# A pad of 224 bytes behind the small parameters of a hybrid decoder step

## What is computed

```python
h = rmsnorm(x, p['norm1_g']) * (1.0 + sc1[:, None]) + sh1[:, None]
mo, st = mixer(h, tuple(s[l] for s in states), lb_all[l], p)   # h @ w_in, three head groups, @ w_out
x = x + gt1[:, None] * mo
h = rmsnorm(x, p['norm2_g']) * (1.0 + sc2[:, None]) + sh2[:, None]
x = x + gt2[:, None] * peer(h, p['peer_wq'], p['peer_k1'], p['peer_k2'], p['peer_u'], p['peer_v'])
```

```python
act = jax.nn.gelu(jnp.einsum('thkd,td->thk', jnp.take(u, idx, axis=0), xb).astype(jnp.float32))
return jnp.einsum('thk,thkd->td', (gw * act).astype(xb.dtype), jnp.take(v, idx, axis=0))
```

## The kernel before

| tensor | start | modulo 64 | modulo 512 |
|---|---|---|---|
| x_res | 16512 | 0 | 128 |
| ring | 25728 | 0 | 128 |
| parts | 38016 | 0 | 128 |
| keep | 50304 | 0 | 128 |
| small | 52160 | 0 | 448 |
| mod | 54560 | 32 | 288 |
| gain, cond, rms, sel | 56288 to 59040 | 32 | |
| big | 63648 | 32 | 160 |
| x_parts, h_parts, act_parts, extra_ring, onehot | 210592 | 32 | 160 |
| more_ring | 214688 | 32 | 160 |

## Time and profile before

### The profile page before, as it was taken

The page is one execution under the profiler, slowest core; times in us unless marked ns, Lnnn a source line. Parts: engine busy times, 40 slices in busy tenths (PEclk is TensorE's granted clock), DMA queues, the critical chain, the costliest instruction groups (busy, mean ns, idle before and its releaser), DMA issues. The chain is left out here.

```text
span 2366.9 us, 58299 instructions
## 1 busy us (share of the span) xinstructions
PE 2266.2 (96%) x20478; PEld 2076.5 (88%) x20478; DVE 1494.1 (63%) x3095; ACT 1268.8 (54%) x2439; POOL 1054.6 (45%) x960
## 2 busy tenths in 40 slices
PE   6989999999999999999999799999999999999998
PEld 4955869999998799999989367799999978999997
DVE  3746636963225968888666664299432288787885
ACT  3533215567557955555556322165665587555554
POOL 0010106884446746566300210088644475665661
PEclk8978999999999999999999779999999999999999
DMA  7475034555552079899545821455555502898992
GB/s 281 155 280 201 3 131 164 178 181 202 188 189 92 6 264 312 287 301 312 194 171 170 310 101 38 137 185 178 199 183 187 188 33 91 295 312 275 312 312 100
DMA packets 123806, 455.40 MB, mean 192 GB/s; under 512 B 13744, under 2 KB 14256, under 8 KB 122544
## 3 DMA queue, kind: packets, MB, share of 16 engines
q1 hardware_dynamic: 105264, 386.80, 45.9%
q0 software_dynamic: 18432, 67.12, 10.3%
HBM read 449.37 MB, written 4.49 MB: 192 GB/s over the span
## 5 line engine op out<-in xcount | busy, mean ns | idle before, releaser
L426 POOL TENSOR_TENSOR parts<-ring,parts 128x512 fp32r<-128x512 f32 x358 | 463.9, 1298 | 472.0 <-ACT parts L419 457.6
L419 ACT ACTIVATE parts<-ring 128x512 fp32r<-128x512 f32 x620 | 389.2, 632 | 348.4 <-PE ps_u L473 280.5
L469 PE MATMUL ps_u<-h_parts,parts 128*128 128x256 f32 x4096 | 563.5, 280 | 0.9 <-ACT parts L419 0.6
L2649 PE MATMUL ps_y<-act_parts,parts 128*128 128x256 f32 x4096 | 563.0, 279 | 0.0
L469 PEld LDWEIGHTS ps_u<-h_parts,parts 128*128 128x128 f32 x4096 | 514.4, 188 | 3.1 <-ACT parts L419 1.7
L2649 PEld LDWEIGHTS ps_y<-act_parts,parts 128*128 128x128 f32 x4096 | 515.1, 188 | 0.7 <-ACT parts L2589 0.3
L426 DVE TENSOR_TENSOR parts<-ring,parts 128x512 fp32r<-128x512 f32 x262 | 180.6, 692 | 372.8 <-ACT parts L419 351.1
L2698 POOL TENSOR_TENSOR act_parts<-big,act_parts 128x256 fp32r<-128x256 f32 x256 | 246.5, 963 | 304.4 <-ACT act_parts L2678 304.4
L473 PE MATMUL ps_u<-h_parts,parts 128*128 128x256 f32 x2048 | 322.7, 279 | 1.4 <-DVE parts L426 1.1
L2653 PE MATMUL ps_y<-act_parts,parts 128*128 128x256 f32 x2048 | 322.3, 279 | 0.0
L473 PEld LDWEIGHTS ps_u<-h_parts,parts 128*128 128x128 f32 x2048 | 275.2, 188 | 2.2 <-DVE parts L426 1.5
(11 more groups left out here) (398 smaller groups left out, 2813.1 us busy)
## 6 DMA issues: line engine op xcount, KB each, us to landing
ring<-in_stream SPq DMA_DIRECT2D x522, 512.0 KB, 3.4
more_ring<-in_stream SPq DMA_DIRECT2D x126, 512.0 KB, 4.9
extra_ring<-in_stream SPq DMA_DIRECT2D x48, 512.0 KB, 5.8
big<-in_stream SPq DMA_DIRECT2D x16, 512.0 KB, 11.7
out_state_out<-big SPq DMA_DIRECT2D x2, 1440.0 KB, 7.0
big<-in_state SPq DMA_DIRECT2D x2, 1280.0 KB, 10.1
big<-in_mixc SPq DMA_DIRECT2D x2, 1024.0 KB, 7.7
big<-in_spots SPq DMA_DIRECT2D x2, 1024.0 KB, 5.5
```

Of the source, the lines that this page charges most:

```text
L419: eng.activation(m.parts[:, q % PARTS, 0, :], half_tile(m, t, half), ACT.Copy).then_inc(s["hi_ready"], 1)
L426: eng.tensor_tensor(m.parts[:, q % PARTS, 1, :], half_tile(m, t, half), m.parts[:, q % PARTS, 0, :].bitcast(F32), ALU.subtract).then_inc(m ...
L469: pe.matmul(out, hi[:, k, :], hr[:, side, kk, 0:tokens], start=(kk + side == 0), stop=False)
L2649: pe.matmul(ps[:, half * KD // 2 + k, :], hi[:, k, :], act_parts[:, j % AHEAD, side, :], start=False, stop=False)
```

## The change

One tensor of 56 float32 values per partition (224 bytes) is named behind `small`. Nothing reads or writes it. All that is named after it starts 224 bytes higher; `x_res`, `ring`, `parts`, `keep` and `small` stay where they are.

```diff
         self.keep = sb("keep", [P, KEEP_W])
         self.small = sb("small", [P, SMALL_W])
+        self.line_end = sb("line_end", [P, 56])
         self.mod = sb("mod", [P, 6 * KD, 1 + NB])
         self.gain = sb("gain", [P, 2, KD, 1 + NB])
         self.cond = sb("cond", [P, KD, COND])
```

## The result

The changed kernel takes **2408.67 us** (median of 4 runs, 2405.88 to 2416.36) against 2372.0 us for the kernel before (median of 4, 2367.56 to 2381.35). The ratio is 1.0164, with a 95% interval of 1.0135 to 1.0193: slower by 1.6%, where a gain of 1.7% was forecast. The two medians are 36.7 us apart, which is 1.5% and lies in that interval, too. The profiled execution took 2409.18 us with a span of 2407.2 us, 40.3 us more than before.

The account below looks back on a forecast made before the run. TensorE, busy for 96% of the span, was taken to bound the kernel. The profiled 2368.9 us less 36.9 and 3.9 gave 2328.1 us; with the runs' median 4.5 us higher, 2332 us was predicted, range 2300 to 2390 us.

Parts of the forecast that it names:

- step 2: Expert products, `h_parts` and `act_parts` at their new start: 3 ns gained on each of 12288 matmuls, 36.9 us.
- The first line of the earlier trace: Projection matmul durations spread from 291 to 298 ns around 296, read as a sign that addresses matter.
- Rival B: Expert matmuls: memory repeats every 256 bytes, new offset worse by 1.3 to 2 ns each, 16 to 25 us lost; 20%.
- lower bound of step 2: Expert products: nothing gained, or 1.3 to 2 ns a matmul lost, 16 to 25 us.
- The upper bound: Expert products: at most 4.7 ns a matmul gained, 57.8 us, taken from the one-hot products' pace of 112 ns.
- Rival A: Expert matmuls: the 10 ns surplus is weight handover, not addresses; time stays within a few us of 2373; 30%.
- Rival C: Expert blocks: pace reaches 112 ns or less, but GpSimd, VectorE or DMA hold tiles back; 2345 to 2355 us; 7%.
- Step 1: The pad itself: no instruction touches it, it costs space only, 0 us.
- Step 3: Input projection, `x_parts` slices all moved to multiples of 64: 3 ns a matmul gained, 3.9 us.
- Steps 4 and 5: Plain float32 products, then other engines and DMAs, at new addresses: 0 us each.
- The two paces of the earlier trace: experts_block ran at 116.8 ns a matmul in layer 0 and 118.1 in layer 1, read as rhythms of two conflicting read streams.

Follow-up runs that it names:

- experiment 1: Small kernel without the computation, float32r matmuls at thirty-eight places: with 256 columns, distance 256 gave 288 cycles a matmul, distance 32 gave 282.6 or 280.2.
- experiment 3: The changed kernel with a pad of 256 bytes instead of 224: 2370.98 us, ratio 0.999 against the kernel before.
- experiment 8: Small kernel without the computation, places around distance 112 and 288 columns: 112 and 368 gave 272.0 cycles, 108 and 116 gave 288 or more.
- experiment 9: The kernel before with `h_parts` and `act_parts` begun 80 bytes into larger tensors, making distance 112: 2334.65 us, ratio 0.9841.
- experiment 12: Small kernel without the computation, distances 0, 32 and 112 with 128, 64 or 32 weight columns, and plain float32: the latter 518 cycles at all three.

## Why the prediction was wrong

**The step that failed is number 2**, "The value I take is 3 ns gained". Measured: 3.33 ns lost on each of the 12288 matmuls, 41 us the other way. The inference behind it was that a row which shows that places differ also says that another place is a better one. It says only that. The best and the worst place were equally open, and I had no row for distance 256. I gave the pad's two properties a value for being there: the multiple of 64 is none (experiment 1), and "off a multiple of 512" has a meaning only modulo 256, where 256 is the same as 0. The first line of the earlier trace rows was also a poor ruler for size, as it comes from 288 columns, which have a table of their own. The second line, of 256 columns, was the better one: its durations of 277 to 282 ns are single matmuls of one steady stream, and from 600 us on their starts in the kernel before are 113, 116, 118 and 120 ns apart, over and over, which is 116.7 ns in the mean. The best and the worst pace found later, 113.3 and 120.0 ns, stood in it side by side, 3.3 ns to either side. (From 405 us on the starts are 116 and 117 ns apart, so the unevenness is a hint, and no rule.)

**Rival B had it, with the wrong price.** Its mechanism was a memory that repeats every 256 bytes, so that the new distance is the worse one, at the start of each matmul. The period is measured (experiments 1, 3 and 8), and so is the loss. That both streams start in one part of a memory is only its picture: no run shows the parts, and distance 96, 104 or 248 is as slow as 0 or slower. Its price, 1.3 to 2 ns, was the highest that the rows of before showed for a second pace; the measured one is 3.33 ns, so that 2389 to 2398 us became 2409 us, past the end of the range. The lower bound of step 2 should not have been taken from differences seen at other places. The upper bound was taken widely, from another kind of matmul, and the lower one narrowly: a lower bound as wide as the upper, 4.7 ns a matmul and 58 us, would have held the time.

**Rival A is refuted** as it was put, with a time that stays: by distance alone the kernel's pace goes from 272 to 288 cycles. The 16 cycles of surplus that are left at the best place may still be what it says; no run shows that. **Rival C** was not put to the test by the change, since nothing was gained. In experiment 9 the covers held at 113.3 ns; its own condition, 112 ns or less, was never reached.

**By steps.** Step 1 (the pad itself, 0 us): held, by experiment 3. Step 3 (the projection, 3.9 us gained): wrong in sign, by 3.4 us lost from first to last matmul, 1.5 us of them busy time. The step said that only the multiple of 64 could be gained, and it was nothing. The slices' distances went from 32 and 160 (modulo 256) to 0 and 128. Experiment 1 has 316 and 319.8 cycles there, 132.5 ns in the mean, which would be no slower than the 132.8 ns of before; measured were 133.3 ns in layer 0 and 136.1 ns in most of layer 1. So the small kernels don't give the projection's pace, where four slices with two distances follow each other, and its loss is open. Steps 4 and 5 (0 us): held, as far as can be told beside the shifts of the clock. The queries still go on at 242 ns, as in the earlier trace rows, though their distance changed, and experiment 12 shows the same for 256 columns: plain float32 doesn't feel it. The one-hot products, still at 112 ns, say nothing on it, as both their operands lie in `onehot` and keep their distance.

**One reading was too large.** The prediction put the expert products at 1771.5 us and 75% of the span. That is the sum of four groups that overlap; 12288 x 116.7 ns is 1434 us, 61%. The terms of the sum were counted by matmuls, so none of them hangs on it.

**The two paces of the earlier trace rows** were read rightly as rhythms of one stream: 280 and 282.7 cycles are the two paces of distance 32. **The upper bound** of 4.7 ns held: experiment 9 gains 3.33 ns. That its 2334.65 us stand where I had put the change is luck. The 3 ns came from two rows of other kinds of matmul, and the 3.9 us of the projection are in neither kernel.

**What was used of the Trainium skill.** The measurement decides against the rule of two independent read ports (the Trainium skill, "TensorE: Matmul & The Clock Gate", "Step-by-step: what each phase is for") as I used it: by it the change would have brought 0 us, and it cost 37. Whether the two operands' reads meet in those ports, or in something behind them, no run shows. N / 2.4 + 2.5 ns (the Trainium skill, "TensorE: Matmul & The Clock Gate", "Back-to-back issue gap"), which that section gives for the isolated gap and not for a stream with a weight load each, fits plain float32 with 256 columns in experiment 12 all the same, 6 cycles or 2.5 ns over its 512. For float32r the best of all places was 113.3 ns against its 109.2. The unit of 16 bytes (the Trainium skill, "SBUF — State Buffer", "Specifications (TRN2)") is not the one that counts: steps of 4 bytes (108, 112, 116) move the pace by 16 cycles.

**What stays open** is the mechanism: why 112 and not 108, why the table changes with the number of columns and with weights off a multiple of 32, what sets 272 cycles, the lowest seen with 256 columns, and what slows the projection. 272 is 17/16 of 256, and 512 columns at distance 256 gave 544, again 17/16. I have no run that explains it.

## What to carry to other kernels

Where one core runs float32r matmuls back to back, lay the distance between moving operand and weights modulo 256 bytes as deliberately as the loops, and **measure it, don't reason it**. Small kernels with 48 matmuls per place gave the paces that every pad of the expert blocks could have here, and their 288, 280 and 272 cycles were those of the whole kernel; for the projection they didn't. Look at the starts of single matmuls in a steady stretch, too: how unevenly they follow each other was the better bound in both directions here than rows of another kind of matmul. Look for a place that has one pace and not two, for the column count in use, with the weights on a multiple of 32 bytes; and when a row shows only that places differ, give the unseen place equal bounds on both sides.

## What was new of the hardware

- The pace of float32r matmuls with 256 columns depends on the distance of the two operands with a period of 256 bytes: 272 to 311 cycles. From 272 to 288 is 41 us, or 1.7% of this kernel's time.
- Some distances have two steady paces (64: 272.0 and 282.7; 192 as well; 32: 280.2 and 282.6), and what ran before decides. At distance 64 one block took 364 us in one layer and 351 us in the other, and the whole kernel's runs spread over 30 us (2349.69 to 2379.62), of which the clock accounts for a part.
- The good place is 4 bytes wide: 112 gives 272.0, 108 and 116 give 288 and more. It holds with weights at 0, 32, 64 and 128 behind a multiple of 128 and is lost at 4, 8, 16 and 48.
- Another column count has another order: with 288 columns, 112 is among the slowest places, and with 512, distance 32 is slower than 256 (560 against 544 cycles).
- Plain float32 with 256 columns has 6 cycles of surplus at each of the three distances tried (0, 32 and 112).
